# RWKV layer with 32 experts and two attention mixers on one core: one large zero fill instead of 32, one matrix product and one weight fetch moved

## The chip, the core and the metric

The kernel is one program on one NeuronCore of a Trainium2 chip, everything in float32. The metric is the device time of one execution in microseconds (us). The kernel before takes 3712.61 us, the median of three executions (3710.7, 3712.61 and 3723.88).

The engines work side by side, each through a list of instructions of its own, and wait for one another by semaphores: PE (TensorE) does matrix products, its weight loads are shown apart as PEld; DVE (VectorE), ACT (ScalarE) and POOL (GpSimd) do elementwise work; SP (SyncE) issues transfers. Transfers are issued from three engines here. SP and ACT have one queue each, q1 is SP's and q10 is ACT's; POOL's gathers are q0. All of them share the core's 16 DMA engines.

## The reference

1,024 tokens of 1,024 numbers pass through one layer (a pooling mixer and RWKV-7 heads, then a mixture of 32 experts) and two attention layers (grouped queries, then a latent one), both with an adaptive norm whose scales come from a product of a condition with `w_mod`. Cut to what matters here:

```
# mixture: top group, top 2 experts in it; the rows are sorted by expert and padded to blocks
ys = lax.map(expert_block, (row_tok, row_w, block_expert))     # silu(xb @ gate[e]) * (xb @ up[e]) @ down[e]
return zeros((n, d)).at[row_tok].add(ys.reshape(m_pad, d))     # each token: its two rows of ys
# attention layer
shift, scale, gate = split(silu(c) @ w_mod + b_mod, 3)         # w_mod 1024 x 3072
h = rms_norm(x, norm_w) * (1 + scale) + shift
k, v, q, g = split(h @ p["w_in"], cuts)                        # k and v: the first 512 columns
k = rope(rms_norm(k, k_norm)); q = rope(rms_norm(q, q_norm))
```

## The kernel before, in words

`program` runs through stages: `mixers` (until about 880 us), `out_and_norm` (output projection, first norm, until about 1005), `experts` (routing until about 1042, then the experts until about 1436), the combination of the experts' rows together with the keys of the first attention layer (the class `Combine` and the keys), and the two attention layers.

**The order of work is written out by hand.** Each stage builds a list of steps, and `walk` hands each step to the programs of PE, ACT, DVE, POOL and SP in turn. A step's instructions so stand on every engine in the place that the list gives them; an engine that must wait holds all that stands behind it.

**Mixers.** The RWKV heads are worked two at a time, in six pairs f = 0 to 5. For each pair come `zr`, `fill`, `rk`, then the triangular inverses (`merges`), the scan over chunks (`scan`, with its step `scan_y` for c = 0 to 7), and beside these the projections of the next pair. ACT copies results out of PSUM between PE's products: line 680 at the end of `rk`, line 686 in the merges, line 701 at the end of a scan half.

**Zeroing `d_ys`.** The experts write their rows into the buffer `d_ys` in HBM (4,096 rows of 4 KB, 16.8 MB), and the combination gathers two rows for each token. Blocks without tokens aren't written, so the whole buffer is zeroed ahead. In `scan_y` of f = 0 to 3 (line 697) ACT issues 32 transfers of 512 KB, in packets of 1 KB, from a tile of zeros. SP waits for their semaphore `cleared` before its first store of an expert's rows (line 1828).

**Routing and the modulation.** While DVE works out which token goes to which expert, PE does the first products of the condition with `w_mod`, in parts i = 0 to 5 of 512 columns. The weights of part i (2 MB, packets of 2 KB) are fetched by ACT into one of two buffers (line 1120, `act_fetch`); `pe_product` (line 1137) multiplies 8 slices of them, `act_gather` (line 1146) copies the bank out, `pe_fold` (line 1151) adds the four parts, DVE adds the bias and ACT stores the row to `d_mod`. `pe_rows` (line 1579) is the routing's product: it turns the one-hot places of the tokens, which DVE makes (line 1571), into row numbers, for which the first gathers and the first transposes of the experts (`turn`, line 1720) wait.

**Experts.** There are 32 slots (`SLOTS`), each with two pieces of 64 rows. For a slot s, PE does `gu` (line 1732, gate and up), `hid` (line 1741) and `down` (line 1752). An expert's weights are three pieces of 1 MB, double-buffered. SP issues them by `sp_fetch`: at the step `gu` of slot s the gate and up weights of slot s + 2 (line 1674), at its `down` the down weights of s + 2 (line 1678), and then the stores of slot s's rows (line 1828). A fetch whose expert is the one already in the buffer is skipped by a condition; such an issue is in the trace as one of 0.08 us.

**The steps called `ahead`** bring in the first attention layer. `ahead` 1 is SP's alone (lines 2243 to 2245): `wkv`, the key and value columns of `in_l_w_in` (2 MB, 1,024 packets of 2 KB), and the two rows `q_norm` and `k_norm`, each copied to 128 partitions (128 packets of 256 B). They are first used by the key products (line 2400). `ahead` 2 loads the context rows, `ahead` 5 transposes them on PE. The step `mod` of slot 28 fetches the modulation's parts 4 and 5 on ACT's queue.

Of the kernel before, what the change touches and what calls it, by code (L numbers as in the profile page):

```python
# [16 lines left out]
P = 128  # L17
S = 1024
D = 1024
# [3 lines left out]
SLOTS = 32  # L23
HALVES = 2 * SLOTS
HROWS = 64
# [168 lines left out]
def mixers(k, a, dr, c_tok):  # L194
# [174 lines left out]
    order += k_next + [("pool_mm", 1)] + weave(r_next, decay(0) + [("kk", 0), ("kk_sq", 0)])  # L369
    order += prepare(0, ([], project(6) + [("shift", 6, "vT")]))  # L370
    for f in range(6):
        order += [("zr", f, 1)] + fill(f) + [("rk", f)]
        beside = (finish(f - 1) if f else []) + tail(f)
        if f < 5:
            k_next, r_next = kr(f + 1)
            beside = weave(beside + decay(f + 1), k_next + r_next[:8]) + [("kk", f + 1), ("kk_sq", f + 1)]
            order += weave(weave(merges(0), merges(1)), beside)
            order += prepare(f + 1, (scan(f, 0) + scan(f, 1), r_next[8:] + project(9 + 3 * f) + [("shift", 9 + 3 * f, "vT")])) + [("scan_end",)]
        else:
            order += [("ahead", 0)] + weave(weave(merges(0), merges(1)), beside) + [("ahead", 1)]  # L380
            order += weave(scan(f, 0) + scan(f, 1), [("out", n, half, kk) for kk in range(7) for n in range(2) for half in range(2)])
            order += [("scan_end",)] + weave(finish(f)[:-1], [("out", 2, half, kk) for half in range(2) for kk in range(7)])
# [212 lines left out]
    def act_program(kind, *x):  # L595
# [19 lines left out]
        elif kind == "tanh":  # L615
            act.wait_ge(*t["shift", "wd"])
            act.e.activation(wd[0:64, :], wd[0:64, :], ACT.Tanh).then_inc(*act_out.up())
            t["wd"] = act_out.at
        elif kind == "sigm":
            act.wait_ge(*t["shift", "gd"])  # L620
            act.e.activation(gd, gd, ACT.Sigmoid).then_inc(*act_out.up())
            t["gd"] = act_out.at
        elif kind == "pool_z":
            act.wait_ge(*t["poolout"])
            for half in range(2):
                act.wait_ge(*t["proj", half])
                act.e.activation(T[0][:, half_of(half)], k.bank(6 + half), ACT.Copy).then_inc(*evac_a.up())
                free[6 + half] = t["z"] = evac_a.at
        elif kind == "lora_mm":
            f, half = x  # L630
            for tok in t["prep_end"]:
                act.wait_ge(*tok)
            act.wait_ge(*t["lora"])
            act.e.activation(T[0][:, half_of(half)], k.bank(4), ACT.Sigmoid, bias=pc[:, 20 + f:21 + f])
            act.e.activation(T[1][:, half_of(half)], k.bank(5), ACT.Sigmoid, bias=pc[:, 26 + f:27 + f]).then_inc(*act_out.up())
            free[4] = free[5] = t["sigs"] = act_out.at
        elif kind == "kk_sq":
            act.wait_ge(*t["kk"])
            act.e.activation(sq, T[2], ACT.Square).then_inc(*act_out.up())
            t["sq"] = act_out.at  # L640
        elif kind == "kk_rsqrt":
            act.wait_ge(*t["kkn"])
            act.e.activation(T[3], T[3], ACT.Ln).then_inc(*act_out.up())
            act.wait_ge(*act_out.at)
            act.e.activation(T[3], T[3], ACT.Exp, scale=-0.5).then_inc(*act_out.up())
            t["kkr"] = act_out.at
        elif kind == "decay_p":
            fc = fcs[x[0] % 2]
            act.wait_ge(*t["fcp"])
            act.e.activation(fc[:, 16:24], fc[:, 8:16], ACT.Exp, scale=-CDEC).then_inc(*act_out.up())  # L650
            t["fc", x[0]] = act_out.at
        elif kind == "exps":
            act.wait_ge(*t["ctr"])
            act.e.activation(T[0], T[0], ACT.Exp, scale=-CDEC).then_inc(*act_out.up())
            t["ex"] = act_out.at
            act.wait_ge(*t["kn"])
            act.e.activation(T[3], T[4], ACT.Exp, scale=-CDEC).then_inc(*act_out.up())
            t["ep"] = act_out.at
            act.e.activation(T[4], T[4], ACT.Exp, scale=CDEC).then_inc(*act_out.up())
            t["em"] = act_out.at  # L660
        elif kind == "tail_turn":
            f, n = x
            if n % 2:
                dst = (Bt, Kt, Vt)[n // 2]
                b = 4 + n % 2
                act.wait_ge(*t["tailturn"])
                act.wait_ge(*t["scan_end"])
                act.e.activation(dst[:, 4:8, :], k.bank(b).rearrange("p (j t) -> p j t", j=4), ACT.Copy).then_inc(*evac_a.up())
                free[b] = t["tok1"] = evac_a.at
        elif kind == "ab":  # L670
            c, = x
            v = k.ps[:, 3072:4096].rearrange("p (h t) -> p h t", h=2)
            up, low = halves
            act.wait_ge(*t["zbmm"])
            j = 2 * (c % 4)
            act.e.activation(zb[c // 4][up, j, :], v[up, 0, 0:128], ACT.Copy)
            act.e.activation(zb[c // 4][low, j, 0:64], v[low, 0, 64:128], ACT.Copy).then_inc(*evac_a.up())
            free[6] = evac_a.at
            act.e.activation(zb[c // 4][low, j + 1, :], v[up, 1, 0:128], ACT.Copy)
            act.e.activation(zb[c // 4][up, j + 1, 0:64], v[low, 1, 64:128], ACT.Copy).then_inc(*evac_a.up())  # L680
            free[7] = t["zb", c // 4] = evac_a.at
        elif kind == "merge_a":
            g, lv = x
            if lv:
                act.wait_ge(*t["mm", g])
                act.e.activation(by_head(Ms, g), M_(g), ACT.Copy).then_inc(*masked.up())
                t["M free", g] = t["Ms", g] = masked.at
        elif kind == "join_a":
            g, = x
            act.wait_ge(*t["mm", g])  # L690
            act.e.activation(by_head(Ms, g)[64:128], M_(g)[64:128], ACT.Copy).then_inc(*masked.up())
            t["M free", g] = t["Ms", g] = masked.at
        elif kind == "scan_y":
            f, c = x
            if f < 4:
                act.wait_ge(*t["zero"])
                act.e.dma_start(dr["ys"].rearrange("(n p) (q c) -> n p q c", p=P, c=256)[8 * f + c], bc(zero, 1, D // 256)).then_inc(*cleared.up(16))
            if c % 4 == 3:
                act.wait_ge(*t["ym"])
                act.wait_ge(*t["yfree"])  # L700
                act.e.activation(yT[:, 512 * (c // 4):512 * (c // 4) + 512], k.bank(5), ACT.Copy).then_inc(*act_out.up())
                free[5] = t["y"] = act_out.at
        elif kind == "fin_sq":
            f, half = x
            act.wait_ge(*t["ycen", half])
            act.wait_ge(*t["mix"])
            act.e.activation(fsq[:, half_of(half)], yT[:, half_of(half)], ACT.Square).then_inc(*act_out.up())
            t["ysq", half] = act_out.at
        elif kind == "fin_ln":
            f, half = x  # L710
            act.wait_ge(*t["vard", half])
            act.e.activation(fsq[:, half_of(half)], fsq[:, half_of(half)], ACT.Ln).then_inc(*act_out.up())
            t["lnd", half] = act_out.at
        elif kind == "fin_exp":
            f, half = x
            act.wait_ge(*t["lnd", half])
            act.e.activation(fsq[:, half_of(half)], fsq[:, half_of(half)], ACT.Exp, scale=-0.5).then_inc(*act_out.up())
            t["rstd", half] = act_out.at
# [638 lines left out]
def experts(k, a, dr, c_tok, mod, keys):  # L1357
# [252 lines left out]
    mod.act_fetch(3)  # L1610
    mod.act_gather(0, 3)
    mod.pe_fold(0, 3)
    mod.act_gather(1, 4)
    mod.pe_fold(1, 4)
    t_dst = dve_places(counted)
# [4 lines left out]
        mod.act_store(i)  # L1620
        mod.act_fetch_bias(i + 2)
    t_turn = pe_rows(t_hots)
    mod.pe_product(2, 5)
    mod.act_gather(2, 5)
    mod.pe_fold(2, 5)
    mod.pe_product(3, 6)
# [64 lines left out]
    for s in range(SLOTS):  # L1691
        order.append(("gu", s))
        if s == SLOTS - 2:
            order.append(("ahead", 2))
        if s == SLOTS - 1:
            order.append(("ahead", 3))
        if s:
            order.append(("down", s - 1))
        if s == SLOTS - 2:
            order.append(("ahead", 1))  # L1700
        if s == SLOTS - 1:
            order += [("ahead", 6), ("ahead", 4)]
        tail = [("hid", s)] + ([("turn", s + 2)] if s + 2 < SLOTS else [])
        order += tail if s else tail[::-1]
        if s == 2:
            order.append(("ahead", 0))
        if s == SLOTS - 4:
            order.append(("mod", s))
    order += [("ahead", 5), ("down", SLOTS - 1)]

    def pe_program(kind, s):
# [2080 lines left out]
```

## Time and profile before

| | |
|---|---|
| time, median of three executions | 3712.61 us |
| the profiled execution's own time | 3723.88 us |
| its span in the trace | 3722.1 us |
| TensorE's mean granted clock in it | 0.976 of full speed |
| busy: PE, PEld, DVE, ACT, POOL | 3506.6, 2009.9, 1643.7, 1166.7, 489.6 us |
| chain that ended last | PE 84%, DVE 8%, DMA 2%, ACT 2%, issue 2% |
| bytes of the two queues | q1 231.91 MB, q10 42.05 MB |

The busy times are sums over the span, so PE with 3506.6 us in 3722.1 us works 94% of it. The chain follows the work that ended last back to the start, step by step, to what released each step; its shares say which engine's time made up the span. A timeline row gives start and duration in us, then engine, line, operation and the tiles; in square brackets stands how long the engine had been idle before, and what released it. The row of a transfer on SPq or ACTq is the time that the issuing engine spent on issuing it, not the transfer itself.

### The profile page before, as it was taken

What the parts mean: (1) busy time and instruction counts of PE and PEld (TensorE: products, weight loads), DVE (VectorE), ACT (ScalarE), POOL (GpSimd) and SP (SyncE); (2) the same over time, 40 slices, a digit from 0 to 9 for tenths busy, and PEclk for the clock granted to TensorE, in tenths of its full rate; (3) what the DMA queues carried; (4) which work ended last, traced back from release to release, by engine and by line L of the source; (5) the groups of instructions that cost most, each with busy time, mean ns of one, the idle gap of its engine ahead of it and who ended that gap; (6) DMA issues with size and microseconds to landing.
All of it is one profiled execution on the core that took longest, in us unless ns stands there. A gap on an engine that the chain in (4) does not pass through costs nothing.

```text
span 3722.1 us, 57094 instructions
## 1 busy us (share of the span) xinstructions
PE 3506.6 (94%) x24253; PEld 2009.9 (54%) x24253; DVE 1643.7 (44%) x2564; ACT 1166.7 (31%) x2075; POOL 489.6 (13%) x476
## 2 busy tenths in 40 slices
PE   8899999989889998989999999998998999899999
PEld 4465565565433333445555555555554666566654
DVE  2454555453321114724445445443225655455541
ACT  1333333321111112433333333342213444344430
POOL 0222121211110002301011011101102000200000
PEclk9999999989799999999999999999999999999999
DMA  3011012031379989900000000030200000000001
GB/s 111 24 63 64 23 54 69 13 117 46 146 306 347 380 302 388 304 12 17 18 18 18 1 18 18 12 111 23 81 6 12 1 1 14 15 9 1 1 24 67
DMA packets 115396, 302.77 MB, mean 81 GB/s; under 512 B 13142, under 2 KB 55446, under 8 KB 101958
## 3 DMA queue, kind: packets, MB, share of 16 engines
q1 hardware_dynamic: 78470, 231.91, 17.1%
q10 hardware_dynamic: 29760, 42.05, 3.1%
q0 software_dynamic: 6912, 25.17, 1.8%
q8 instruction: 191, 3.13, 0.3%
q14 instruction: 63, 0.52, 0.0%
HBM read 345.71 MB, written 55.10 MB: 108 GB/s over the span
## 4 chain that ended last, share of the span: by engine, by line
PE 84%; DVE 8%; DMA 2%; ACT 2%; issue 2%; POOL 1%; SPq 1%; ACTq 0%; DVEq 0%; POOLq 0%
PE ps L2716 11%; PE ps L2162 8%; PE ps L408 8%; PE ps L2191 8%; PE ps L3428 7%; PE ps L1732 6%; PE ps L2734 4%; PE ps L1194 3%; PE ps L3700 3%; PE ps L3109 3%; PE ps L1752 2%; PE ps L3381 2%; PE ps L2400 1%; PE ps L504 1%; DMA sb<-in_exp_up 1%
## 5 line engine op out<-in xcount | busy, mean ns | idle before, releaser
L2716 PE MATMUL ps<-sb 128*128 128x512 f32 x960 | 467.1, 606 | 19.6 <-ACT sb L2074 10.9
L2162 PEld LDWEIGHTS ps<-sb 128*128 128x128 f32 x2624 | 290.0, 142 | 305.2 <-ACT sb L2170 130.0
L2162 PE MATMUL ps<-sb 128*128 128x128 f32 x2624 | 419.5, 283 | 19.4 <-DVE sb L2178 9.6
L2170 ACT ACTIVATE sb<-ps 128x512 f32<-128x512 f32 x336 | 200.1, 597 | 716.5 <-PE ps L2162 716.5
L2136 ACT ACTIVATE sb<-ps,sb 128x1280 f32<-128x1280 f32 (+1 forms) x288 | 353.2, 1231 | 130.5 <-DVE sb L2129 111.9
L2178 DVE COPY sb<-ps 128x512 f32<-128x512 f32 x320 | 220.0, 689 | 379.4 <-PE ps L2162 378.8
L408 PE MATMUL ps<-sb 128*128 128x512 f32 x704 | 352.9, 618 | 4.6 <-DMA sb<-in_w_in 3.0
L3428 PE MATMUL ps<-sb 96*128 96x512 f32 (+1 forms) x768 | 332.7, 526 | 8.7 <-DVE sb L3485 7.2
L2191 PEld LDWEIGHTS ps<-sb 128*64 128x64 f32 x5248 | 287.3, 138 | 70.0 <-issue 39.8
L2191 PE MATMUL ps<-sb 128*64 128x128 f32 x5248 | 321.8, 277 | 3.3 <-DVE sb L2178 3.1
L1957 POOL TENSOR_TENSOR sb<-sb 128x1 f32<-128x1 f32 (+3 forms) x114 | 131.9, 1158 | 1062.2 <-DVE sb L1953 1062.1
L2125 DVE TENSOR_REDUCE sb<-ps 128x1 f32<-128x1024 f32 (+1 forms) x192 | 200.8, 1046 | 129.0 <-PE ps L3428 124.5
L2115 DVE TENSOR_REDUCE sb<-ps 128x2 f32<-128x2560 f32 (+1 forms) x80 | 191.8, 2397 | 147.5 <-PE ps L2734 147.4
L1732 PE MATMUL ps<-sb 128*64 128x512 f32 x1024 | 229.9, 602 | 9.5 <-DMA sb<-in_exp_up 9.5
L2716 PEld LDWEIGHTS ps<-sb 128*128 128x128 f32 x960 | 164.1, 193 | 137.0 <-issue 110.4
L408 PEld LDWEIGHTS ps<-sb 128*128 128x128 f32 x704 | 120.2, 191 | 103.9 <-issue 96.5
L2734 PE MATMUL ps<-sb 64*128 64x256 f32 (+1 forms) x832 | 170.2, 538 | 5.2 <-ACT sb L2136 3.4
L1732 PEld LDWEIGHTS ps<-sb 128*64 128x64 f32 x1024 | 72.3, 138 | 143.0 <-issue 139.5
L2734 PEld LDWEIGHTS ps<-sb 64*128 64x128 f32 x832 | 98.5, 190 | 92.9 <-issue 80.8
L3428 PEld LDWEIGHTS ps<-sb 96*128 96x128 f32 x768 | 121.6, 191 | 14.4 <-DVE sb L3485 7.7
L1005 POOL TENSOR_TENSOR sb<-sb 128x512 f32<-128x512 f32 x72 | 96.6, 1360 | 210.1 <-ACT sb L680 131.9
L1799 DVE TENSOR_TENSOR sb<-sb,ps 128x256 f32<-128x256 f32 x32 | 13.5, 421 | 244.9 <-ACT sb L1775 244.9
(373 smaller groups left out, 4576.2 us busy)
## 6 DMA issues: line engine op xcount, KB each, us to landing
sb<-in_exp_gate SPq DMA_DIRECT2D x65, 1024.0 KB
sb<-in_exp_up SPq DMA_DIRECT2D x65, 1024.0 KB
sb<-in_exp_down SPq DMA_DIRECT2D x65, 1024.0 KB
sb<-in_l_w_mod ACTq DMA_DIRECT2D x12, 2048.0 KB, 14.9
d_ys<-sb ACTq DMA_DIRECT2D x32, 512.0 KB, 4.1
d_ys<-sb SPq DMA_DIRECT2D x64, 256.0 KB
sb<-d_x SPq DMA_DIRECT2D x32, 512.0 KB, 3.8
sb<-in_w_in SPq DMA_DIRECT2D x22, 512.0 KB, 4.2
```

The costliest lines, as they stand in the source:

```text
L408: ins = pe.e.matmul(k.bank(6 + half), wt[i % 2][:, kk, :], xT[:, kk, half_of(half)], start=kk == 0, stop=kk == 7)
L1732: ins = pe.e.matmul(v[64 * h:64 * h + 64], xT[b][:, kk, 64 * h:64 * h + 64], gu_of[lane_of(s, h)][:, kk], start=kk == 0, stop=kk == 7, ski ...
L2115: dve.e.tensor_reduce(self.mx[:, i:i + 2], src, AX, ALU.min).then_inc(*self.maxed.up())
L2125: dve.e.tensor_reduce(out, src, AX, ALU.min).then_inc(*self.maxed.up())
L2136: act.e.activation(self.Pb[g % 2][:, self.cols(g, b)], self.k.ps[:, self.cols(g, b)], ACT.Exp, bias=self.mx[:, i:i + 1], scale=-1.0, accum ...
L2162: ins = k.pe.e.transpose(k.bank(bank)[:, 128 * j:128 * j + 128], self.Pb[g % 2][:, 1280 * b + 128 * c:1280 * b + 128 * c + 128], k.f(C_ID, ...
L2170: k.act.e.activation(self.PT[:, xs[0]:xs[-1] + 1, :], k.bank(bank)[:, 0:128 * len(xs)].rearrange("p (j t) -> p j t", j=len(xs)), ACT.Copy) ...
L2178: k.dve.e.tensor_copy(self.PT[:, xs[0]:xs[-1] + 1, :], k.bank(bank)[:, 0:128 * len(xs)].rearrange("p (j t) -> p j t", j=len(xs))).then_inc ...
L2191: ins = k.pe.e.matmul(k.bank(7)[64 * b:64 * b + 64, o:o + 128], values(c, b), self.PT[:, nk * b + c, :], start=c == 0, stop=c == nk - 1, s ...
L2716: ins = pe.e.matmul(k.bank(5), lhs[:, kk, :], w[:, kk, 512 * half:512 * half + 512], start=kk == 0, stop=kk == 7)
L2734: ins = pe.e.matmul(k.ps[:, 1280 * b + lo:1280 * b + hi], qT[hs, aa, j, :], kT[hs, aa, lo:hi], start=True, stop=True, skip_group_check=True)
L3428: ins = pe.e.matmul(k.ps[:, 1280 * b + lo:1280 * b + hi], qT[0:96, h, :], kT[:, h, lo:hi], start=True, stop=True, skip_group_check=True)
```

## The change

It has three parts.

1. The 32 zeroing transfers in `scan_y` are gone. Instead a step `clear` stands behind `rk` of pair 1, ahead of that pair's merges, in which ACT issues one transfer over all of `d_ys`: 128 partitions by 128 packets of 1 KB, 16,384 packets in one instruction.
2. In the routing, `mod.pe_product(2, 5)` stands between `pe_fold(0, 3)` and `act_gather(1, 4)`, no longer behind `pe_rows`.
3. `ahead` 1 stands behind the step `mod` of slot 28, no longer behind `down` 29 in slot 30.

```diff
     for f in range(6):
-        order += [("zr", f, 1)] + fill(f) + [("rk", f)]
+        order += [("zr", f, 1)] + fill(f) + [("rk", f)] + ([("clear",)] if f == 1 else [])
...
+        elif kind == "clear":
+            act.wait_ge(*t["zero"])
+            act.e.dma_start(dr["ys"].rearrange("(p r) (q c) -> p (r q) c", p=P, c=256), bc(zero, 1, HALVES * HROWS * D // (256 * P))).then_inc(*cleared.up(16))
...
         elif kind == "scan_y":
             f, c = x
-            if f < 4:
-                act.wait_ge(*t["zero"])
-                act.e.dma_start(dr["ys"].rearrange("(n p) (q c) -> n p q c", p=P, c=256)[8 * f + c], bc(zero, 1, D // 256)).then_inc(*cleared.up(16))
...
     mod.pe_fold(0, 3)
+    mod.pe_product(2, 5)
     mod.act_gather(1, 4)
...
     t_turn = pe_rows(t_hots)
-    mod.pe_product(2, 5)
     mod.act_gather(2, 5)
...
             order.append(("down", s - 1))
-        if s == SLOTS - 2:
-            order.append(("ahead", 1))
         if s == SLOTS - 1:
...
         if s == SLOTS - 4:
-            order.append(("mod", s))
+            order += [("mod", s), ("ahead", 1)]
```

ScalarE at the end of `rk` of pair 1, before (the names in brackets are semaphores, `product` is raised by PE, `dve_out` by DVE):

```order
L676 ACTIVATE sb<-ps 64x128 [waits product]
L677 ACTIVATE sb<-ps 64x64
L679 ACTIVATE sb<-ps 64x128
L680 ACTIVATE sb<-ps 64x64
L707 ACTIVATE sb<-sb 128x512 [waits dve_out]
L686 ACTIVATE sb<-ps 128x2x4x64 [waits product]
```

And after, where the line numbers of this place are higher by 3 up to 694:

```order
L679 ACTIVATE sb<-ps 64x128 [waits product]
L680 ACTIVATE sb<-ps 64x64
L682 ACTIVATE sb<-ps 64x128
L683 ACTIVATE sb<-ps 64x64
L639 DMA d_ys<-sb 16384x1x256
L707 ACTIVATE sb<-sb 128x512 [waits dve_out]
L689 ACTIVATE sb<-ps 128x2x4x64 [waits product]
```

The single zeroing transfer (L639) stands ahead of the copies of the merges.

TensorE in the routing, before (`mod_part` is raised by `act_gather`, `modw_in0` by the landing of part 2's weights, `dve_out` by the one-hots for `pe_rows`):

```order
L1137 MATMUL ps<-sb 32x512 x8
L1151 MATMUL ps<-sb 2x512 [waits mod_part] x2
L1579 MATMUL ps<-sb 64x32 [waits dve_out]
L1579 MATMUL ps<-sb 64x32 x31
L1137 MATMUL ps<-sb 32x512 [waits modw_in0]
L1137 MATMUL ps<-sb 32x512 x7
L1151 MATMUL ps<-sb 2x512 [waits mod_part]
```

After:

```order
L1137 MATMUL ps<-sb 32x512 x8
L1151 MATMUL ps<-sb 2x512 [waits mod_part]
L1137 MATMUL ps<-sb 32x512 [waits modw_in0]
L1137 MATMUL ps<-sb 32x512 x7
L1151 MATMUL ps<-sb 2x512 [waits mod_part]
L1579 MATMUL ps<-sb 64x32 [waits dve_out]
L1579 MATMUL ps<-sb 64x32 x31
L1151 MATMUL ps<-sb 2x512 [waits mod_part]
```

The product of part 2 and its wait for weights now stand ahead of the second fold and of `pe_rows`.

SP in the last slots, before, between the stores of slot 29 and those of slot 30 (`evac_a` and `evac_v` are raised when the rows are copied out):

```order
L1828 DMA d_ys<-sb 64x1024
L2243 DMA sb<-in_l_w_in 128x8x512
L2244 DMA sb<-in_l_q_norm 128x64
L2245 DMA sb<-in_l_k_norm 128x64
L1827 TENSOR_LOAD sb [waits evac_a,evac_v]
L1827 ISA x2
L1828 ISA
L1828 DMA d_ys<-sb 64x1024
```

After, in slots 28 and 29, where line numbers are lower by 2 (`product` is raised by the `gu` that frees the buffer):

```order
L1826 DMA d_ys<-sb 64x1024
L2241 DMA sb<-in_l_w_in 128x8x512
L2242 DMA sb<-in_l_q_norm 128x64
L2243 DMA sb<-in_l_k_norm 128x64
L1669 TENSOR_LOAD sb
L1669 ISA x2
L1670 TENSOR_LOAD sb
L1670 ISA x2
L1674 ISA [waits product]
L1674 DMA sb<-in_exp_gate 128x2048
L1674 DMA sb<-in_exp_up 128x2048
```

The three loads of `ahead` 1 now stand right behind the stores of slot 27 and right ahead of the gate and up weights of slot 31, the last slot. DVE's and POOL's orders are what they were.

## Rows read from the trace of the kernel before

**Rows 1.** The page's first line.

```profile
span 3722.1 us, 57094 instructions
```

**Rows 2.** Transfers issued at line 697: issue in ns, min/median/max; then landing.

```profile
L697 ACTq DMA_DIRECT2D d_ys<-sb x32: 541/566/1091, 212.5 to 615.0; - x32
...
DMA to landing us min/median/max: 3.2/4.1/6.0
```

**Rows 3.** Timeline of ScalarE, line 701 in the scans of pairs 1 to 4.

```profile
380.56 0.60 ACT L701 ACTIVATE sb<-ps 128x512 f32<-128x512 f32 x1 [13.61 <-PE ps L569]
...
504.14 0.60 ACT L701 ACTIVATE sb<-ps 128x512 f32<-128x512 f32 x1 [13.61 <-PE ps L569]
...
629.34 0.60 ACT L701 ACTIVATE sb<-ps 128x512 f32<-128x512 f32 x1 [13.61 <-PE ps L569]
...
752.92 0.60 ACT L701 ACTIVATE sb<-ps 128x512 f32<-128x512 f32 x1 [13.61 <-PE ps L569]
```

**Rows 4.** Windows: span, busy PE, PEld, DVE, ACT, POOL, clock, DMA share, GB/s.

```profile
242.60:246.60 4.00, 4.00 (x25) 2.70 (x25) 0.87 (x4) 0.78 (x1) 1.77 (x2) 1.00 0.97 340
```

**Rows 5.** Timeline of ScalarE, end of `rk` and first merge of pair 1.

```profile
272.99 0.22 ACT L680 ACTIVATE sb<-ps 64x64 f32<-64x64 f32 x1
...
279.48 0.60 ACT L686 ACTIVATE sb<-ps 128x512 f32<-128x512 f32 x1 [2.57 <-PE ps L485]
```

**Rows 6.** Timeline of SP's issues from 262 to 360 us, its weight loads.

```profile
318.24 35.83 SPq L300 DMA_DIRECT2D sb<-in_w_in  x2
```

**Rows 7.** Transfers issued at lines 300 and 1120: issue in ns, min/median/max.

```profile
L300 SPq DMA_DIRECT2D sb<-in_w_in x22: 539/540/5801, 10.8 to 690.6; - x22
...
L1120 ACTq DMA_DIRECT2D sb<-in_l_w_mod x12: 547/548/767, 930.5 to 1511.2; - x12
```

**Rows 8.** Timeline of ScalarE in the routing: fetch of part 2, its gather.

```profile
1011.98 0.55 ACTq L1120 DMA_DIRECT2D sb<-in_l_w_mod  x1
...
1037.40 0.60 ACT L1146 ACTIVATE sb<-ps 128x512 f32<-128x512 f32 x1 [16.68 <-DMA d_mod<-sb]
```

**Rows 9.** Queues from 1015 to 1029.5 us: packets, MB, share of 16 engines.

```profile
q10 hardware_dynamic: 1124, 2.27, 41.3%
```

**Rows 10.** Timeline of TensorE: `pe_rows`, the product of part 2, `gu` of slot 1.

```profile
1029.90 3.63 PE L1579 MATMUL ps<-sb 128*64 128x32 f32 x64 [7.73 <-DVE sb L1571]
1033.46 3.00 PE L1137 MATMUL ps<-sb 128*32 128x512 f32 x16
...
1059.91 8.60 PE L1732 MATMUL ps<-sb 128*64 128x512 f32 x32 [5.16 <-DMA sb<-in_exp_up]
```

**Rows 11.** Timeline of SP's issues in the last slots.

```profile
1400.22 1.82 SPq L1828 DMA_DIRECT2D d_ys<-sb  x2
...
1425.18 4.10 SPq L2244 DMA_DIRECT2D sb<-in_l_q_norm  x1
...
1437.46 2.23 SPq L1828 DMA_DIRECT2D d_ys<-sb  x2
```

**Rows 12.** SP's queue from 1381 to 1409.6 us.

```profile
q1 hardware_dynamic: 1501, 10.16, 88.5%
```

**Rows 13.** Both queues from 1431 to 1434 us, both with packets of 2 KB.

```profile
q1 hardware_dynamic: 279, 0.59, 52.8%
q10 hardware_dynamic: 280, 0.57, 50.8%
```

**Rows 14.** SP's queue from 1410 to 1416 us, packets of 8 KB, beside ACT's.

```profile
q1 hardware_dynamic: 274, 1.97, 78.1%
```

**Rows 15.** Timeline of TensorE: `gu` of slot 31, the key products, the next gap.

```profile
1419.88 7.09 PE L1732 MATMUL ps<-sb 128*64 128x512 f32 x32
...
1440.93 8.83 PE L2400 MATMUL ps<-sb 128*128 128x512 f32 x16 [3.13 <-DMA sb<-in_l_w_in]
...
1466.19 1.87 PE L1151 MATMUL ps<-sb 128*2 128x512 f32 x2 [5.47 <-ACT sb L1146]
```

**Rows 16.** Timeline of GpSimd: first gather of the experts' rows.

```profile
1445.56 1.00 POOL L1880 DMA_INDIRECT sb<-d_ys,sb  x1 [15.07 <-DMA d_ys<-sb]
```

## The prediction, made before the changed kernel ran

> **What bounds the kernel.** I read the page's shares first: TensorE works 94% of the span and makes most of the chain that ended last, so an edit counts only where it makes PE wait, or ends a wait of PE. The traffic of the page's DMA row is far from full over the whole, but full in the last slots of the experts. So for each part I asked, in the timelines of PE, ACT and SP, which wait ends last at that place, and in the views of the queues what the DMA engines moved there. The sum is made against the profiled execution, 3723.88 us with a span of 3722.1 [rows 1]. It is the longest of the three executions before, 11.3 us over their median of 3712.61; I carry the difference over to the median unchanged.
>
> **Part 1, the zeroing.** Gone are 32 issues of 0.57 us on ACT [rows 2], 18 us of its time. They are worth nothing, and the kernel itself holds the comparison: pair 2's scan issues eight of them, pair 4's none. From the end of pair 1's scan to that of pair 2's it is 504.14 − 380.56 = 123.58 us, from pair 3's to pair 4's 752.92 − 629.34 = 123.58 us [rows 3]. Before that instruction ACT had been idle for 13.61 us in all four. (Pairs 2 to 3 took 125.20; both have clears beside the scan in question, so that is something else.) The cover is ACT's idle time.
>
> Added is one issue, at about 273.2 us, behind line 680 [rows 5]. An issue of 1,024 packets takes 0.54 us at its fastest and one of 512 packets the same [rows 2, 7]: it does not grow with packets, so I take 0.6 us. Behind it stands the copy of the first merge at 279.48, idle before for 2.57 us [rows 5]: it hides. Next, the traffic. A clear moves its 1 KB packets at 340 GB/s with the engines' share at 0.97 [rows 4]; 16.8 MB take 16.78 / 0.340 = 49 us, from 273 to 322. In that stretch SP issues weight loads, a group of two that begins at 318.24 [rows 6]; the second comes 35 us later, and the buffers are loaded ahead by about that much. The first shares the engines for 4 us and may land 4 us later, of a slack of 35. Cost 0. If the cover were gone, it would be those 4 us; and nothing below 0 is to be had, since the clears cost nothing where they were. The stores of expert rows, which wait for `cleared`, come over 700 us later.
>
> The price that this leaves open is how long ACT is held when one instruction carries 16,384 packets. An issue can be held: one of line 300 took 5.80 us against 0.54, and the `q_norm` issue 4.10 [rows 7, 11]. Bounds: 0.54 us, and the whole time until its packets have nearly drained, about 43 us. The nearest rows are the loads of `w_mod` with 1,024 packets, issued two in a row: never over 0.77 us [rows 7], although the first of two was hardly begun. I take 0.6 and keep the other as a rival. 
>
> **Part 2, the product of part 2.** Its weights are issued at 1011.98 [rows 8]. ACT's ring moves 1,124 packets from 1015 to 1029.5 [rows 9], and the product needs 1,024 of them, behind some small ones: they are through at about 1029.5. PE had been idle for 7.73 us until 1029.90, when the one-hots were ready [rows 10]. The move looks as if it filled this gap, but the weights come only at its end. So: product 1029.5 to 1032.5 (3.0 us, [rows 10]), the fold of part 1 behind it to 1033.0, then `pe_rows`, 3.6 us, to 1036.7, where it ended at 1033.5 before. It is late by 3.2 us, and the product's place behind it is empty. The row numbers follow late by at most these 3.2 us (they were copied behind the product's wait before, so in fact by some 0.5). ACT's gather of part 2 waited for a store of `d_mod`, to 1037.40, 16.68 us [rows 8], and does so still. Whatever reaches slot 0 meets the 5.16 us that PE waits before `gu` of slot 1, for `in_exp_up`, a transfer [rows 10]: it absorbs −3.0 and +3.2 alike. Taken: 0. Bounds: −3.0, the product's own time; +3.2.
>
> **Part 3, `wkv` ahead of the last slot's weights.** This moves three issues past two stretches of SP's queue.
>
> - *When SP gets there.* Behind the stores of slot 27, 1400.22 + 1.82 = 1402.04 [rows 11]. Before it was 1424.5.
> - *What lies ahead in the ring.* From 1381, when it was empty, to 1409.6 SP's queue moved 10.16 MB [rows 12]. Issued by 1402.04 are nine pieces of 1.05 MB and three stores of 0.26 MB that weren't skipped, 10.2 MB. So `wkv` begins to move at about 1409.6.
> - *Its own time.* ACT's queue is moving `w_mod` parts in packets of 2 KB then. Where both queues had packets of 2 KB they moved one for one, 279 and 280 in 3 us [rows 13], 93 a microsecond each. `wkv` is 1,024 packets: 11.0 us, to 1420.6. The two norm rows are 256 small packets, 1.6 us at about 160 a microsecond (the 2 KB rows would give 2.8): 1422.2.
> - *Then the weights of slot 31*, gate and up of its one live piece, 2 x 128 packets of 8 KB. Beside ACT's queue SP's moved 274 packets in 6 us [rows 14], 45.7 a microsecond: 5.6 us, and with the landing 0.5 more: 1428.4.
> - *What PE does.* `gu` of slot 31 began at 1419.88 and waited for nothing [rows 15]. Now it waits until 1428.4: 8.5 us. After a wait PE is slower for a while: the same 32 products took 8.60 us behind a 5.16 us wait and 7.09 us without one [rows 10, 15]. With these 1.5 us the last `down` is late by 10.
> - *What comes back.* `wkv` has landed long before the first key products, whose wait of 3.13 us (and 8.83 us for work of 7.13) goes. But 20 us behind them PE idles for 5.47 us for ACT's gather [rows 15], and the combination, not PE, sets the pace: it starts with the gather of expert rows at 1445.56, which had waited 15.07 us for `d_ys` [rows 16]. This gather depends on the last stores. Their issue ended at 1439.69 [rows 11], and they landed 5.9 us later; SP's ring is emptier now, since `wkv` is gone from it, and the clears landed in 3.2 to 4.1 us [rows 2]. So about 2 us come back: +10 − 2 = +8.
>
> Bounds of part 3: 0, if the slot's weights aren't delayed beyond the 3.9 us between their landing (1409.6 + 5.6 + 0.5, about 1416) and their use, and if the key wait counted, −5; on the other side +13, if `wkv` moves at two thirds of that rate (16.5 us). The same page of the Trainium skill, section "Rules for kernel authors", says to issue a transfer early, compute, and wait late. By that rule this part only removes the 3.13 us and the slow clock's 1.7 and gives −4.8; it is part of the rival "faster" below. The rows say the opposite here, since one ring serves first what was issued first, and the early one stands ahead of a transfer that is needed sooner.
>
> **The sum.** 0 + 0 + 8 = +8 us: 3731.9 for the profiled execution, 3720.6 for the median. I forecast 3721.
>
> **The rivals.**
>
> - *ACT is held by the large transfer* (slower). ACT would be let go when about 1,400 packets are left: 15,000 at 340 a microsecond, 44 us behind 273.2, at 317. The first copy of the merges stood at 279.48: late by 37 us, and PE with it, as PE waits for every such copy. Decides: an issue longer than 6 us. With part 3's 8 us: 3757. For it: the 5.80 us row. Against it: the pairs of 1,024 packets.
> - *Nothing moves* (3713). `wkv` is served fast enough, or the ring is emptier at 1402 than I count, and slot 31's weights come by 1420. It decides at 8 us of delay of that ring, which would need 2,048 packets of both queues in 8 us, 256 a microsecond where the rows show 186.
> - *Faster* (3705). The key wait of 3.13 us, its slow clock of 1.7 and the 3.0 of the moved product all lie on the path: −7.8. For it: PE does wait at all three places. It decides if the weights of slot 31 still come in time and the 5.47 us gap behind the keys closes with the earlier keys. Against it: the gap behind is longer than the wait before, and ends by another engine.
>
> **How the numbers follow.** The forecast has 0.66, ACT held 0.12, nothing moves 0.15, faster 0.07. The forecast's own range is 3714 to 3730: its bounds, 0 and +13, with about 3 us of what a median of few executions moves. The range for all reaches to the faster and the unmoved case and a little above the bounds: 3706 to 3736, and leaves out the held case. Half a per cent is 18.6 us, about what a measurement of this kernel can tell from no change: below 3694 nothing but an unknown remains, 0.04; above 3731.2 the held case and the upper tail of the forecast, 0.12 + 0.06 = 0.18; the rest is 0.78.
>
> **What would show it.** Line 639's issue of 0.5 to 0.6 us, a burst of 49 us in ACT's queue behind 273, and the first merge copy still at 279.5. `pe_rows` starting 3 us later behind the product, and `gu` of slot 1 at 1059.9 still ending a DMA wait. In slot 31 `gu` behind a wait of about 8.5 us for `in_exp_gate` or `in_exp_up`, ended at 1428.4, no wait at the first key product, and the first gather of expert rows about 8 us later. I am wrong if PE waits in the merges of pair 1, or if `gu` of slot 31 starts within 2 us of 1419.9.

## The result: slower by 20 us, where 8 were forecast

The changed kernel takes 3740.57 us, the median of five executions (3729.87 to 3743.48), beside 3721.29 for the kernel before on the same chip (3710.7 to 3723.88). The ratio is 1.0055, with a 95% interval of 1.0032 to 1.0078: +20.5 us, from 11.9 to 29.0. The range given was 3706 to 3736. Of the 19.6 us between the 3721 that I forecast and 3740.57, 8.7 are the base: the median of before is 3721.29 in these runs and was 3712.61 in the three that I had. The other 10.9 are the change's. The sign was right, the size was not, and the larger share of the loss stands in a part that was put at nothing. Of all executions behind the ratios below one, of part 2 alone, took 10,528 us; its ratio leaves it out.

The profiled execution is 3731.61 us with a span of 3729.8, only 7.7 us over that of before. The spans mislead here. In the attention layers, which no edit touches, the trace of before fell 16 us behind that of the changed kernel; the traces of the experiments, which change nothing there either, gained on it in the same way, by 6 to 16 us. So I compare stretch by stretch, by when the same instruction begins.

**Part 1: 10 us lost in the merges of pair 1.** The issue took 0.68 us and ACT was not held. These are the transfer's rows, the same view as [rows 2]:

```profile
L639 ACTq DMA_DIRECT2D d_ys<-sb x1: 682/682/682, 272.9 to 272.9; - x1
...
DMA to landing us min/median/max: 51.5/51.5/51.5
```

And this is the timeline of ScalarE at the ends of the scans of pairs 1 and 2, which answers to [rows 3]:

```profile
391.10 0.60 ACT L701 ACTIVATE sb<-ps 128x512 f32<-128x512 f32 x1 [13.61 <-PE ps L569]
...
514.71 0.60 ACT L701 ACTIVATE sb<-ps 128x512 f32<-128x512 f32 x1 [13.61 <-PE ps L569]
```

Pair 2 takes 123.61 us, as before (123.58). Pair 1 ends at 391.10, not 380.56: 10.5 us late, of which 0.7 were there before the burst. The waits of TensorE from 280 to 330 us name the cause. In the kernel before this stretch has no line with "issue":

```profile
PE ps L485 <- issue: 4.6, 2, 2.8
PE ps L495 <- issue: 1.0, 1, 1.0
PE ps L504 <- issue: 0.3, 1, 0.3
```

"Issue" means that the profile shows nothing that TensorE waited for. I read it as: its next instruction wasn't there. The timeline of PE gives the places:

```profile
288.14 0.39 PE L495 MATMUL ps<-sb 64*64 64x64 f32 x10 [1.04 <-issue]
...
302.04 1.55 PE L485 MATMUL ps<-sb 64*64 64x64 f32 x55 [2.85 <-issue]
303.51 3.08 PE L408 MATMUL ps<-sb 128*128 128x512 f32 x4
...
315.83 0.35 PE L485 MATMUL ps<-sb 64*64 64x64 f32 x2 [1.73 <-issue]
316.11 3.61 PE L408 MATMUL ps<-sb 128*128 128x512 f32 x4
```

The rows of L408 behind an idle are the second half of the price: the same four products take 1.98 us elsewhere in this stretch. The windows show the clock (columns: span, busy PE, PEld, DVE, ACT, POOL, granted clock, share of the DMA engines, GB/s):

```profile
282.00:292.00 10.00, 8.96 (x177) 5.17 (x170) 3.18 (x5) 1.43 (x3) 3.87 (x4) 1.00 1.03 348
292.00:302.00 10.00, 7.19 (x176) 4.81 (x176) 3.27 (x5) 4.62 (x6) 1.76 (x2) 1.00 1.03 349
302.00:312.00 10.00, 9.96 (x207) 6.35 (x210) 3.65 (x7) 1.62 (x3) 2.51 (x2) 0.83 1.03 351
```

From 302 on the mean granted clock is 0.83, the share of a mix of 2.4 and 1.2 GHz, after a stretch in which PE was busy 7.19 of 10 us. So 5.9 us of idle and about 4 of slow clock (0.17 of two such windows, 302 to 322, is 3.4).

**Where instructions come from.** The page has a queue q8 of the kind "instruction": 191 packets, 3.13 MB, so 16 KB each. PE has 24,253 products and as many weight loads, 254 for each packet, and 256 with its 475 semaphore and drain instructions. So a packet is a block of TensorE's program, and it travels over the same 16 DMA engines as the zeros. The queues of the changed kernel from 285 to 320 us:

```profile
q10 hardware_dynamic: 11861, 12.15, 102.0%
q8 instruction: 5, 0.08, 0.8%
```

The kernel before, from 281 to 316, the same work:

```profile
q8 instruction: 7, 0.11, 1.4%
```

By the single packets' records, blocks began 4.1 to 6.1 us apart before, and in the burst 6.9, 6.9, 7.0, 6.8 and 7.0. The idles end 2.2 to 2.5 us after such a packet begins (285.9, 299.7, 313.5, 320.4). The merges need 939 products and weight loads in 20 us, 47 a microsecond; a block of 254 every 6.9 us brings 37.

Where the idles stand says more than when. The four idles for issue stand behind 4,288, 4,800, 5,313 and 5,569 of PE's instructions (products, weight loads, semaphores): 512, 513 and 256 apart, two blocks, two blocks, one. In the traces of the experiments below, part 1 alone has its idles behind the same four instructions, the four transfers have their only one behind 4,800, and the quarters theirs behind 4,288. TensorE ran out at the ends of blocks.

The kernel before has one such idle itself, in the merges of pair 5, which I had overlooked. From 799 to 807 SP's five loads of 512 KB, in packets of 4 KB, fill the DMA engines (the window and the timeline of PE):

```profile
799.00:807.00 8.00, 5.02 (x236) 4.67 (x234) 2.82 (x5) 1.21 (x2) 0.00 (x0) 1.00 0.94 324
```

```profile
805.79 0.86 PE L504 MATMUL ps<-sb 64*64 64x64 f32 x22 [2.19 <-issue]
```

The block for it began at 803.3, 8.1 us behind the one before it, and the idle stands behind 17,345 instructions, 51 blocks and 1 instruction behind the first of the four above. So a burst needs neither packets of 1 KB nor 49 us to cost something.

**Part 2: nothing, as forecast.** TensorE's timeline, the product of part 2, `pe_rows`, and `gu` of slot 1 [rows 10]:

```profile
1043.35 3.44 PE L1137 MATMUL ps<-sb 128*32 128x512 f32 x16 [8.40 <-DMA sb<-in_l_w_mod]
...
1047.57 2.06 PE L1579 MATMUL ps<-sb 128*64 128x32 f32 x64
...
1073.58 8.85 PE L1730 MATMUL ps<-sb 128*64 128x512 f32 x32 [5.57 <-DMA sb<-in_exp_up]
```

The product waited for its weights in place of the one-hots, and the wait for `in_exp_up` stayed, with 5.57 us. By the copies of ACT the trace is 13.6 us behind that of before at the first gather of the routing (line 1146) and 13.9 in the first slots. It had been 10.5 at the end of pair 1; the 3.1 us between are hardly the change's, since the traces of part 3 alone and of the run at slot 24, which keep parts 1 and 2 as before, fall behind by 2.9 in the same stretch.

**Part 3: a wait of 11.5 us, of which 5 came back.** SP's issues [rows 11]:

```profile
1416.20 0.63 SPq L2241 DMA_DIRECT2D sb<-in_l_w_in  x1
1416.88 6.14 SPq L2242 DMA_DIRECT2D sb<-in_l_q_norm  x1
1423.06 1.34 SPq L2243 DMA_DIRECT2D sb<-in_l_k_norm  x1
1425.84 0.34 SPq L1674 DMA_DIRECT2D sb<-in_exp_gate  x1
```

TensorE: `gu` of slot 31, the two first key products, the gap behind [rows 15]; and GpSimd's first gather [rows 16]:

```profile
1445.71 8.81 PE L1730 MATMUL ps<-sb 128*64 128x512 f32 x32 [11.54 <-DMA sb<-in_exp_up]
...
1465.29 7.13 PE L2398 MATMUL ps<-sb 128*128 128x512 f32 x16
...
1490.77 1.87 PE L1151 MATMUL ps<-sb 128*2 128x512 f32 x2 [7.40 <-ACT sb L1146]
```

```profile
1470.14 1.00 POOL L1878 DMA_INDIRECT sb<-d_ys,sb  x1 [12.08 <-DMA d_ys<-sb]
```

Behind `gu` of slot 31 the trace is 27.6 us behind that of before, where it had been 14.2; on the combination's copies it is 22.6. So +13.4, of which 5.0 came back: +8.4. Of the 5.0, 3.0 were back at the fold behind the gap (1490.77 − 1466.19 = 24.6), about the length of the key wait.

The stretches sum to 9.9 + 0 + 8.4 = 18.3 us, within the interval of the times.

### The profile page after: what moved, and what is told of

The parts are those of the page before. It is cut to its first block, busy times and chain, and to the rows that moved or that the text cites. A ratio compares the mean times of both kernels' runs of the same rounds, so it can differ in the third digit from the quotient of the medians.

```text
span 3729.8 us, 57063 instructions
## 1 busy us (share of the span) xinstructions
PE 3496.4 (94%) x24253; PEld 2003.2 (54%) x24253; DVE 1644.6 (44%) x2564; ACT 1167.6 (31%) x2075; POOL 490.4 (13%) x476
## 3 DMA queue, kind: packets, MB, share of 16 engines
q8 instruction: 191, 3.13, 0.3%
## 4 chain that ended last, share of the span: by engine, by line
PE 83%; DVE 8%; ACT 3%; DMA 2%; issue 2%; SPq 1%; POOL 1%; ACTq 0%; DVEq 0%; POOLq 0%
PE ps L2714 11%; PE ps L408 8%; PE ps L2160 8%; PE ps L2189 7%; PE ps L3426 7%; PE ps L1730 5%; PE ps L2732 4%; PE ps L1194 3%; PE ps L3698 3%; PE ps L3107 3%; PE ps L1750 2%; PE ps L3379 2%; DMA sb<-in_exp_up 2%; PE ps L2398 2%; PE ps L504 1%
## 5 line engine op out<-in xcount | busy, mean ns | idle before, releaser
L2714 PE MATMUL ps<-sb 128*128 128x512 f32 x960 | 461.1, 599 | 19.6 <-ACT sb L2072 10.9
L408 PE MATMUL ps<-sb 128*128 128x512 f32 x704 | 356.0, 623 | 4.7 <-DMA sb<-in_w_in 3.2
L408 PEld LDWEIGHTS ps<-sb 128*128 128x128 f32 x704 | 121.4, 193 | 105.4 <-issue 97.8
```

The lines of the kernel that those rows point to most:

```text
L408: ins = pe.e.matmul(k.bank(6 + half), wt[i % 2][:, kk, :], xT[:, kk, half_of(half)], start=kk == 0, stop=kk == 7)
L2714: ins = pe.e.matmul(k.bank(5), lhs[:, kk, :], w[:, kk, 512 * half:512 * half + 512], start=kk == 0, stop=kk == 7)
```

## The experiments

Each is the kernel before with the edit named. Differences are in microseconds against it on the same chip, with the 95% interval of the ratio.

### Part 1 alone, and the same bytes in four transfers

The first takes the `clear` lines of the diff alone. The second issues four transfers at the same place:

```diff
+            for n in range(4):
+                act.e.dma_start(dr["ys"].rearrange("(n p r) (q c) -> n p (r q) c", n=4, p=P, c=256)[n], bc(zero, 1, ...
```

> Part 1 alone. Starvation theory (mine, formed on the changed kernel's trace): while the 49 us burst of 1 KB packets fills the DMA engines, TensorE's own instruction blocks of 16 KB (256 instructions, queue q8) come only every 6.9 us instead of 5 to 6, and in the merges of pair 1, where TensorE needs more than 37 instructions a microsecond, it runs dry: idles put down to issue of about 5 to 6 us in sum between 286 and 323 us, a clock dip behind them, the end of pair 1's scan 10 us later than before, the whole slower by 8 to 12 us. Rival, drift: the 10 us in the changed kernel's trace were a clock dip of that execution; then the end of pair 1's scan is within 1 us of before, and the time within 3 us.

> As part 1 alone, but the zeroing at that place is four transfers of 4,096 packets each, not one of 16,384; the same bytes, packets and stretch. Starvation theory: the traffic matters, not the number of transfers, so the same 10 us at the same place (8 to 12). Rival, one large transfer is special (its descriptors held at one place): with four the loss is gone or at most a quarter, 0 to 3 us.

Part 1 alone: ratio 1.0020 (1.0007 to 1.0034), +7.4 us (2.6 to 12.6). Its waits of TensorE from 280 to 330 us:

```profile
PE ps L485 <- issue: 4.6, 2, 2.9
PE ps L504 <- issue: 2.0, 1, 2.0
...
PE ps L495 <- issue: 1.0, 1, 1.0
```

7.6 us of idle for issue at the same three lines, and the merges end 9.3 us late. (Its scan of pair 1 loses 2.9 more, with the granted clock at 0.50 from 350 to 354 us; the changed kernel's trace has no such dip.) The loss is that of part 1 and no accident of one trace.

The four transfers: 1.0062 (1.0044 to 1.0081), +23 us. I had expected 10 or nothing; both theories missed, and the timeline of ScalarE shows what I had written off:

```profile
273.70 0.68 ACTq L640 DMA_DIRECT2D d_ys<-sb  x1
...
274.42 8.26 ACTq L640 DMA_DIRECT2D d_ys<-sb  x1
...
282.71 24.44 ACTq L640 DMA_DIRECT2D d_ys<-sb  x2
307.20 0.63 ACT L708 ACTIVATE sb<-sb 128x512 f32<-128x512 f32 x1 [32.47 <-issue]
```

ACT is held, not by a large transfer, but by an issue behind one. By the view of the queues 2,586 packets had begun when the second transfer was let go at 282.7, and 10,863 when the fourth was, at 307.2. Ahead of the second stood 4,096, so 1,510 were left, and ahead of the fourth 12,288, so 1,425. Three transfers more and the rival that I had given 0.12 would have been the truth. It also hid the starvation, as PE's waits from 260 to 380 us show:

```profile
PE ps L495 <- ACT sb L690: 23.7, 1, 23.7
PE ps L485 <- issue: 1.7, 1, 1.7
```

PE stood still for ACT, and blocks could come meanwhile. So this run doesn't settle whether four transfers starve PE as one does.

### The burst beside another stretch, and in four short ones

The one large transfer, first behind the merges of pair 1, ahead of its scan; then four of a quarter, behind `rk` of pairs 0 to 3:

```diff
-            order += weave(weave(merges(0), merges(1)), beside)
+            order += weave(weave(merges(0), merges(1)), beside) + ([("clear",)] if f == 1 else [])
```

```diff
-        order += [("zr", f, 1)] + fill(f) + [("rk", f)]
+        order += [("zr", f, 1)] + fill(f) + [("rk", f)] + ([("clear", f)] if f < 4 else [])
```

> The one large transfer of part 1, but issued behind the merges of pair 1, ahead of its scan (about 322 us instead of 273), where TensorE runs about 12 instructions a microsecond, a third of the 37 at which it would run dry. Starvation theory: no idle put down to issue in the burst, the end of pair 1's scan within 1 us of before, the whole within 3 us of before. Rival, the full DMA engines slow whatever runs beside them (weight loads of the projections that land in the burst, reads and writes of the tiles): 5 to 10 us lost here too, as waits on transfers or longer instructions.

> The one large transfer ahead of the scan of pair 1 once more, since its first runs were 5.6 us below before, with 0.7 as the near end of the interval. If the gain is real (32 issues less beside the scans), the interval again excludes no change, 2 to 8 us below before. If it was chance: within 3 us of before, as my theory has it.

> The zeroing in four transfers of 4,096 packets, one behind rk of each of the pairs 0 to 3, so four bursts of 12 us, each where part 1 has its one burst of 49 us. Starvation theory: in part 1 alone TensorE ran on for 12 to 14 us of burst before its first idle for issue, on instructions already there; bursts of 12 us end before that, so no idle above 1 us in any of the four merges, and the time within 3 us of before. Rival, each microsecond of burst beside merges costs its share (10 us in 49): the same 10 us, 2 to 3 in each pair.

Ahead of the scan: 0.9985 (0.9972 to 0.9998) in the first runs, 0.9997 (0.9983 to 1.0011) in the second: no loss. The −5.6 us of the first lay outside my 3 us; the second (−1.1, from −6.3 to 4.1) leaves open whether there is a small gain. The issue came at 341.4 us, not at about 322. These are the windows of the first, then of the kernel before for the same work:

```profile
345.00:395.00 50.00, 48.08 (x307) 31.14 (x306) 25.97 (x48) 18.37 (x40) 12.55 (x10) 1.00 1.01 342
```

```profile
343.00:393.00 50.00, 48.08 (x307) 31.12 (x306) 25.96 (x48) 18.48 (x40) 12.53 (x10) 1.00 0.29 95
```

The DMA engines are full for 50 us and moved 342 GB/s in place of 95, and PE did the same 307 products in the same 48.08 us. There PE runs 12 instructions a microsecond, a third of what the blocks bring. The two blocks that fell into the burst were late all the same, by 3.3 and 3.9 us against the trace of before, and PE didn't idle, since it had some 200 instructions left when they came. Full DMA engines alone cost nothing beside the scan, which refutes the rival.

The quarters: 1.0005 (0.9991 to 1.0019), +1.9 us (−3.3 to 7.1), no change, and the rival's 10 is excluded. There is one idle for issue in all four merges:

```profile
PE ps L495 <- issue: 1.0, 1, 1.0
```

The same bytes beside merges cost little in four bursts of 12 us and much in one of 49. A burst delays the blocks that fall due in it, and a short one holds few. Short is no safeguard, though: the 8 us of loads in the merges of pair 5 cost an idle of 2.19 us in the kernel before.

### Part 2 alone

Its diff is that of the change.

> Part 2 alone. My theory: the product of part 2 waits for its weights (7 to 8.5 us of waiting for in_l_w_mod instead of the 7.73 us for the one-hots), and pe_rows stands 3 us later; the row numbers, the gathers and slot 0 are where they were within 1 us, the wait before gate and up of slot 1 for in_exp_up is still 5 to 6 us; the time within 3 us. Rival, it carries the rest: the changed kernel lost 20 us and parts 1 and 3 alone 7 and 5, so part 2 costs 5 to 8 us; then the routing ends that much later.

> Part 2 alone once more, for an undisturbed profile. My theory: the product waits 7 to 8.5 us for in_l_w_mod, pe_rows stands 3 us later, the wait before gate and up of slot 1 for in_exp_up is still 5 to 6 us, and slot 1 starts within 1 us of before by the routing's own clock. Rival: it ends 4 us or more later, which would be the 3.7 us by which the first runs of it were over before.

1.0010 (0.9998 to 1.0022) and 0.9996 (0.9978 to 1.0013): no change. This is TensorE's timeline from the second runs:

```profile
1035.96 3.38 PE L1137 MATMUL ps<-sb 128*32 128x512 f32 x16 [8.68 <-DMA sb<-in_l_w_mod]
...
1040.12 2.06 PE L1579 MATMUL ps<-sb 128*64 128x32 f32 x64
...
1065.75 9.02 PE L1732 MATMUL ps<-sb 128*64 128x512 f32 x32 [5.57 <-DMA sb<-in_exp_up]
```

The product of part 0 began 5.7 us later than in the trace of before, and `gu` of slot 1 began 5.8 us later: the routing is as long as it was.

### Part 3 alone, without the norm rows, and earlier

```diff
+        elif j == 7:                      # in slot 30; j == 1 keeps wkv alone
+            sp.e.dma_start(self.qn, a["l0_q_norm_2"]...
```

```diff
+        if s == SLOTS - 7:                # and no longer in slot 30
+            order.append(("ahead", 1))
```

> Part 3 alone. Ring theory: TensorE waits 10 to 12 us before gate and up of slot 31 for in_exp_up, the last down is late by 13, and about 5 come back by the end of the keys (the key wait of 3.1 us and the slow clock behind it are gone, the last stores land sooner): the whole slower by 7 to 10 us. Rival, hidden: the same wait, but all of it comes back, within 2 us of before.

> Part 3 with wkv alone moved; the two norm rows stay behind the stores of slot 29. In the changed kernel their issues held SP for 6.1 and 1.3 us, so that the weights of slot 31 were issued at 1425.8. Ring theory: those weights stand behind wkv in SP's ring in any case; issued 7 us sooner they land at most 2 us sooner, and the wait before gate and up of slot 31 is still 9 to 11.5 us. Rival, SP held: what counts is when SP gets to the issue; the wait falls by 6 to 7 us, to about 5.

> Part 3 with ahead 1 still earlier: behind the stores of slot 24 (about 1365 us), where most fetches are skipped and SP's ring runs empty, and before the modulation's fetches. Ring theory: wkv moves in about 6 us in a gap, no wait before any gate and up from slot 26 to 31 beyond those of before, the key wait of 3.1 us is gone; the time equal to before or up to 4 us less. Rival, any early placement costs its own transfer time somewhere in the experts: 3 to 8 us slower.

Part 3 alone: 1.0013 (1.0002 to 1.0025), +4.8 us (0.7 to 9.3); by its trace +9.7 on the combination's copies. Without the norms: 1.0016 (1.0003 to 1.0029), +6.0; by its trace +8.1. `gu` of slot 31 in the one and in the other:

```profile
1435.11 9.43 PE L1730 MATMUL ps<-sb 128*64 128x512 f32 x32 [11.73 <-DMA sb<-in_exp_up]
```

```profile
1434.20 9.41 PE L1732 MATMUL ps<-sb 128*64 128x512 f32 x32 [10.21 <-DMA sb<-in_exp_up]
```

Without the norms SP began the issue of slot 31's gate weights at 1408.6, not 1414.6. Six microseconds sooner at the queue bought 1.5 at PE. This alone doesn't refute "SP held": the earlier issue was itself held for 4.3 us behind `wkv`, so that the one for `in_exp_up`, which PE waits for, ended only 1.3 us sooner (1414.4, not 1415.7). The records of the single packets decide. The first packet of slot 31's weights began at 1424.3 and 1425.3, 10 to 11 us behind the end of the gate's issue, when `wkv`'s packets (the last at 1427.0 and 1426.1) were almost through. The weights were issued in time and stood in the ring.

Behind the stores of slot 24: 0.9999 (0.9984 to 1.0014). These are SP's issues there, then PE in slot 30 (line 1732) and at the first key product:

```profile
1368.55 0.63 SPq L2243 DMA_DIRECT2D sb<-in_l_w_in  x1
1369.22 0.69 SPq L2244 DMA_DIRECT2D sb<-in_l_q_norm  x1
```

```profile
1412.38 7.09 PE L1732 MATMUL ps<-sb 128*64 128x512 f32 x32
...
1441.10 7.13 PE L2400 MATMUL ps<-sb 128*128 128x512 f32 x16
```

No wait for weights from 1300 to 1440, and none before the key products. Against the trace of before the fold behind the gap comes 3.0 us sooner, and the combination's copies 4.4; traces that keep the key wait drift by up to 1.4 us there. The times leave a gain open, with −6 to +5.

### Both placements together

The large transfer ahead of the scan and `ahead` 1 behind slot 24's stores, without part 2.

> The one large zeroing transfer behind the merges of pair 1 (as in the run with the clear at the scan) and ahead 1 behind the stores of slot 24; part 2 not taken. If both theories hold: no idle for issue beside the burst and no wait for in_exp_up in slot 31, the time 0 to 8 us below before. If either placement still costs: above before.

0.9991 (0.9977 to 1.0005), −3.3 us (−8.6 to 1.9). Its trace has no idle for issue from 260 to 400 us and no wait before `gu` of slot 31, so both losses are gone. The fold behind the gap comes 2.8 us sooner and the copies 2.5. A gain over the kernel before isn't shown by the times.

## Why the prediction was wrong

- **Part 1, the step "Next, the traffic", cost 0: this failed.** I asked only which of the program's own transfers fell into the burst, and wrote that without cover the cost would be 4 us. TensorE's instructions are transfers too: late blocks made PE idle 5.9 us in the merges of pair 1, with about 4 us of slow clock behind, a wait that the sum doesn't have. The part cost 9.9 us in the changed kernel's trace and 7.4 alone. The page of before had the queue q8, with a share of 0.3%; the prediction doesn't name it, nor the idle of 2.19 us in the merges of pair 5. Its own sign of being wrong, PE waiting in the merges of pair 1, came true.
- **The base.** I carried +8 over to a median of three, 3712.61. The median of before is 3721.29 in the result's runs, so 8.7 of the miss are no step of the sum, and the range would have held the result on that base. That is no merit of it: the mechanism of part 1 was missing.
- **The comparison of pairs 2 and 4** [rows 3] was right and was no evidence for this: eight bursts of 1.5 us beside a scan, of 12 instructions a microsecond, say nothing of one of 49 beside merges of 47. Both the length and the neighbour had changed. The merges of pair 5 would have been the place to look.
- **ACT held, 0.12:** didn't happen. The issue of 16,384 packets took 0.68 us. It agrees with the count of descriptors that I cited from the Trainium skill ("DMA: Bandwidth & Descriptors", "Why a DMA increments its semaphore by 16 and not by 1"). The rival's mechanism exists, but for the second large transfer, not the first, as the four transfers showed.
- **Part 2:** right in each step: the wait for the weights (8.40 us where the gap was 7.73), the late `pe_rows` (by 4.1 us, where about 3 were forecast), and the 5 us wait that absorbs it.
- **Part 3:** right in mechanism and net size (+8 forecast, +8.4 by the changed kernel's trace, +4.8 by the times of part 3 alone). That the size fits is luck: two terms were off and cancelled. The wait is 11.5 us, not 8.5. `wkv`'s packets began over 13.3 us (11.0 forecast), and from the last of them to `gu` it was 8.8 us, not 7.8; for the norm rows I took 160 packets a microsecond, while in the trace of before their 256 take 3.2 us, 80 a microsecond. And 5 us came back, not 2: the step that the combination sets the pace, and not PE, was wrong, since the key wait came back with its length (3.0), and 2.0 more on the copies. The Trainium skill's rule to issue early ("DMA: Bandwidth & Descriptors", "Rules for kernel authors") would have given −4.8, and the trace shows +8.4; in the empty ring at slot 24 early did no harm.
- **"Faster", 0.07:** didn't happen. The one thing right in it is the key wait, which I held to be worth little: where it goes, the fold behind the gap comes 2.8 to 3.0 us sooner, nearly the 3.13 us of the wait. The slow clock behind it is worth nothing there, as the gap takes it up, and the moved product nothing either.

Settled by runs: part 1's loss and its place; that the same burst costs nothing beside the scan, and little in four pieces; that TensorE ran dry at the ends of its instruction blocks; that part 3's loss is the order in SP's ring. By the times the parts alone add up to about 12 us (7.4, 0 and 4.8), by the stretches of the trace to 18.3; the whole is 20.5, with 11.9 to 29.0, which holds both. Open: why a block takes 6.9 us in a burst, and what of the traffic delays it. No run moved the same bytes in larger packets, and none changed the instructions' own path. How much slow clock goes with the idles also differs from trace to trace: in the merges about 4 us beside 5.9 of idle in the changed kernel, 1.7 beside 7.6 in part 1 alone.

## What to carry to other kernels

A transfer that nobody waits for still takes the road by which TensorE's instructions come: put a long one beside few, large products, or cut it into bursts with gaps, each of which can still catch a block. A weight needed later must not stand in a ring ahead of one needed sooner, unless the ring is empty there. And a comparison inside the old trace counts only if it keeps the length of the burst and the work beside it.

## What the runs showed of the hardware

- TensorE's program arrives in blocks of 16 KB, some 254 products and weight loads. In a burst of 1 KB packets on all 16 engines a block came each 6.8 to 7.0 us. This capped PE at 37 instructions a microsecond, 18 product and weight pairs.
- Counted in blocks of 256, a block began to arrive at most 302 instructions ahead of its first one in the trace of before (median 264), and at most 157 ahead in the six of the changed kernel's burst, one of them only when PE had used up all that it had. So little stands in reserve.
- The Trainium skill, page "Runtime: NRT & Kernel Launch", section "Instruction fetch mechanics", gives the same blocks of 16 KiB and 256 instructions and calls the fetch mostly hidden. In the merges of pair 1 of the kernel before the trace agrees: no idle for issue. In those of pair 5 (2.19 us) and beside the burst (5.9 us) it doesn't.
- PE ran on for 13 us of burst before its first idle (274.2 to 287.1).
- A DMA issue behind others was let go when 1,425 to 1,510 packets were left ahead of it on ACT's queue, and about 1,170 to 1,200 on SP's (`q_norm` behind `wkv`, in three traces). With nothing ahead 16,384 packets were issued in 0.68 us; 4,096 behind 12,288 were let go only at 307.2.
